# Experts' float32 products written as three products of high and low parts

## The reference

```
hgu = xb @ w_gate_up[e] + b_gate_up[e]
gate, up = jnp.split(hgu, 2, axis=-1)
gate = jnp.minimum(gate, SWIGLU_LIMIT)
up = jnp.clip(up, -SWIGLU_LIMIT, SWIGLU_LIMIT)
act = (up + 1.0) * gate * jax.nn.sigmoid(SWIGLU_ALPHA * gate)
return act @ w_down[e] + b_down[e]
```

## Time and profile before

| | us |
|---|---|
| median of 3 runs | 2881.6 (2881.26 to 2882.64) |
| profiled execution, whole | 2894.67 |
| its span | 2892.9 |
| mean granted TensorE clock in it | 0.948 |

### The profile page before, as it was taken

How to read it: one execution, slowest core, us unless ns; L and a number is a source line. 1 busy time by engine, 2 the same in 40 slices (tenths; PEclk the granted TensorE clock), 3 DMA queues, 4 the chain that set the end, 5 groups by cost and what they waited for, 6 DMA issues and landing times. The chain is left out here.

```text
span 2892.9 us, 47141 instructions
## 1 busy us (share of the span) xinstructions
PE 2727.8 (94%) x18543; PEld 2337.5 (81%) x18544; DVE 1056.3 (37%) x1908; ACT 613.3 (21%) x1272; POOL 242.8 (8%) x214
## 2 busy tenths in 40 slices
PE   7999998786998979999999999999999999999788
PEld 3345543754985559999999999999999999999666
DVE  2143542946242243222223323232323333333365
ACT  2111222325521111111111111111111111111245
POOL 0000001403620000000000000000000000000130
PEclk9999998658999969999999999999999999999889
DMA  3001010000006226677778888899999999999542
GB/s 132 29 30 58 0 62 33 1 22 1 1 19 215 88 84 196 213 234 236 253 257 267 278 265 286 290 296 292 298 295 304 299 309 296 307 298 302 200 158 75
DMA packets 442841, 526.65 MB, mean 182 GB/s; under 512 B 13716, under 2 KB 408808, under 8 KB 442728
## 3 DMA queue, kind: packets, MB, share of 16 engines
q1 hardware_dynamic: 429448, 478.03, 50.4%
q0 software_dynamic: 13280, 46.93, 5.2%
HBM read 486.39 MB, written 38.54 MB: 181 GB/s over the span
## 5 line engine op out<-in xcount | busy, mean ns | idle before, releaser
L1527 PE MATMUL ex_psum<-ex_xT,weight_ring_a 128*128 128x134 f32 (+14 forms) x6144 | 768.9, 286 | 0.8 <-ACT ex_xT L1513 0.8
L1527 PEld LDWEIGHTS ex_psum<-ex_xT,weight_ring_a 128*128 128x128 f32 x6144 | 759.1, 191 | 1.2 <-issue 1.2
L1567 PE MATMUL ex_psum<-ex_hT,weight_ring_b 128*128 128x134 f32 (+14 forms) x4096 | 521.5, 286 | 0.0
L1567 PEld LDWEIGHTS ex_psum<-ex_hT,weight_ring_b 128*128 128x128 f32 x4096 | 508.1, 191 | 0.0
L1537 DVE TENSOR_SCALAR ex_gate<-ex_psum,bias_gate_up 128x192 f32<-128x192 f32 x256 | 95.0, 413 | 696.6 <-PE ex_psum L1527 681.4
L1527 PE MATMUL ex_psum<-ex_xT,weight_ring_b 128*128 128x134 f32 (+14 forms) x2048 | 255.6, 286 | 0.0
L1527 PEld LDWEIGHTS ex_psum<-ex_xT,weight_ring_b 128*128 128x128 f32 x2048 | 252.2, 191 | 0.0
L1541 DVE TENSOR_SCALAR ex_up<-ex_psum,bias_gate_up 128x192 f32<-128x192 f32 x256 | 95.0, 413 | 401.1 <-PE ex_psum L1527 401.1
L239 PE MATMUL project_psum<-nT,w_in_chunks 128*128 128x512 f32 x512 | 225.2, 603 | 3.4 <-DVE nT L358 3.4
L1554 ACT ACTIVATE ex_sig<-ex_gate 128x384 f32<-128x384 f32 x128 | 67.1, 525 | 718.4 <-DVE ex_gate L1537 711.6
L1575 ACT ACTIVATE ex_yT<-ex_psum,bias_down 128x192 f32<-128x192 f32 x256 | 93.8, 418 | 533.0 <-PE ex_psum L1567 533.0
(11 more groups left out here) (313 smaller groups left out, 2908.6 us busy)
## 6 DMA issues: line engine op xcount, KB each, us to landing
weight_ring_a<-in_w_gate_up SPq DMA_DIRECT2D x192, 1024.0 KB, 6.1
weight_ring_b<-in_w_down SPq DMA_DIRECT2D x128, 1024.0 KB, 6.4
weight_ring_b<-in_w_gate_up SPq DMA_DIRECT2D x64, 1024.0 KB, 5.1
y_dram<-ex_y_a SPq DMA_DIRECT2D x33, 512.0 KB, 3.5
w_in_chunks<-in_w_in SPq DMA_DIRECT2D x7, 2048.0 KB, 8.1
y_dram<-ex_y_b SPq DMA_DIRECT2D x33, 256.0 KB, 3.8
project_work<-in_x SPq DMA_DIRECT2D x8, 512.0 KB, 3.7
gates_dram<-project_work POOLq DMA_DIRECT2D x16, 256.0 KB, 2.3
```

The source lines that it names most:

```text
L1527: mm = pe.matmul(self.ps[:, bank, i * CAP:i * CAP + width], w[:, k, i * P:(i + 1) * P], self.xT[:, k, 0:width], start=(k == 0), stop=(k == ...
L1567: mm = pe.matmul(self.ps[:, bank, i * CAP:i * CAP + width], w[:, k, i * P:(i + 1) * P], self.hT[:, k, 0:width], start=(k == 0 and i == 0), ...
```

## The change

Each expert operand exists twice, as a high part (a copy to float32r) and a low part (value minus high part). Every float32 product becomes three float32r products, w_hi by x_hi, w_hi by x_lo and w_lo by x_hi (`pe_product`), and so for h in the down pieces. The host stores the weights piece by piece, so that a partition's 2048 numbers of a piece lie in one run. There are three rings of four pieces: as loaded (`g.raw`), high (`w_hi`, made by ScalarE) and low (`w_lo`, made by VectorE, 1280 or 1024 of the 2048 columns, and by GpSimd, the rest). A piece is loaded when the low part of the piece four before it is made; its high part is made when TensorE has used up the piece four before. x and h are split in the same way by ScalarE and VectorE. TensorE turns y between gate and up pieces, and x in two places before and two between the down pieces. `dve_slots` moves behind the last pass. Freed and taken memory move three loads of `finish` (w_proj and two broadcast rows) into that stage, and w_out of `route` into a tensor of its own.

```diff
-        w_out = g.ring_b[:, 2:6].rearrange("p s n -> p (s n)").rearrange("p (k n) -> p k n", k=KT)
+        w_out = sb("w_out", [P, KT, D])
...
-            for i in range(8):
-                sp.dma_start(ring_slot(g, i).rearrange("p (k n) -> p k n", k=KT), weight_source(g, 0, i)).then_inc(g.w_in_ring[i], 16)
+            for i in range(RING):
+                sp.dma_start(g.raw[:, i], g.w_expert[0, i]).then_inc(g.w_in_ring[i], 16)
...
+RING = 4
+
+LO_CUT = (5 * 256, 4 * 256)
+
+
+def expert_pieces(w_gate_up, w_down):
+
+    up = w_gate_up[0].reshape(E, KT, P, 2, 4, 256).transpose(0, 4, 3, 2, 1, 5).reshape(E, 8, P, 2 * D)
+    down = w_down[0].reshape(E, KT, P, 4, 256).transpose(0, 3, 2, 1, 4).reshape(E, 4, P, 2 * D)
+    return np.ascontiguousarray(np.concatenate([up, down], axis=1))
...
-        self.xT = sb("xT", [P, KT, CAP])
-        self.hT = sb("hT", [P, FF // P, CAP])
+        self.x_hi, self.x_lo = sb("x_hi", [P, KT, CAP], F32R), sb("x_lo", [P, KT, CAP], F32R)
+        self.h_hi, self.h_lo = sb("h_hi", [P, FF // P, CAP], F32R), sb("h_lo", [P, FF // P, CAP], F32R)
+        self.w_hi, self.w_lo = sb("w_hi", [P, RING, 2 * D], F32R), sb("w_lo", [P, RING, 2 * D], F32R)
...
+    def act_x_hi(self, act, x, fill, q, after):
         act.wait_ge(self.turned, fill + q + 1)
-        act.wait_ge(self.gu_done, after)
-        act.copy(self.xT[:, 2 * q:2 * q + 2, :], self.turned_x(q).rearrange("p (i c) -> p i c", i=2)).then_inc(self.turn_kept, 1)
-
-
-    def pe_gate_up(self, pe, m, fill_x, c, width):
-        gate_bank, up_bank = self.GATE_UP[c % 2]
-        if c == 0:
+        if not (isinstance(after, int) and after == 0):
+            act.wait_ge(self.gu_done, after)
+        act.copy(self.x_hi[:, 2 * q:2 * q + 2, :], self.turned_x(q).rearrange("p (i c) -> p i c", i=2)).then_inc(self.x_hi_done, 1)
+
+    def dve_x_lo(self, dve, x, q):
+        cols = slice(2 * q, 2 * q + 2)
+        dve.wait_ge(self.x_hi_done, 4 * x + q + 1)
+        dve.tensor_tensor(self.x_lo[:, cols, :], self.turned_x(q).rearrange("p (i c) -> p i c", i=2),
+                          self.x_hi[:, cols, :].bitcast(F32), ALU.subtract).then_inc(self.turn_kept, 1)
...
+    def act_w_hi(self, act, m, i):
+        act.wait_ge(self.g.w_in_ring[i % RING], 48 * m + 16 * (i // RING + 1))
+        if i >= RING:
+            act.wait_ge(self.gu_done, 8 * m + i - RING + 1)
+        else:
+            act.wait_ge(self.dn_done, 4 * m + i + 1)
+        act.copy(self.w_hi[:, i % RING], self.g.raw[:, i % RING]).then_inc(self.hi_done, 1)
+
+    def w_lo_part(self, eng, m, i, part, done):
+        eng.wait_ge(self.hi_done, 12 * m + i + 1)
+        eng.tensor_tensor(self.w_lo[:, i % RING, part], self.g.raw[:, i % RING, part], self.w_hi[:, i % RING, part].bitcast(F32),
+                          ALU.subtract).then_inc(done, 1)
+
+    def dve_w_lo(self, dve, m, i):
+        self.w_lo_part(dve, m, i, slice(0, LO_CUT[i % 2]), self.lo_dve)
+
+    def pool_w_lo(self, pool, m, i):
+        self.w_lo_part(pool, m, i, slice(LO_CUT[i % 2], 2 * D), self.lo_pool)
+
+    def pe_product(self, pe, out, i, k, slot, hi, lo, width, start, stop):
+        n = slot % RING
+        w_hi, w_lo = (w[:, n].rearrange("p (k n) -> p k n", k=KT)[:, k, i * P:(i + 1) * P] for w in (self.w_hi, self.w_lo))
+        pe.matmul(out, w_hi, hi[:, k, 0:width], start=start, stop=False, skip_group_check=True)
+        pe.matmul(out, w_hi, lo[:, k, 0:width], start=False, stop=False, skip_group_check=True)
+        return pe.matmul(out, w_lo, hi[:, k, 0:width], start=False, stop=stop, skip_group_check=True)
...
-                    mm = pe.matmul(self.ps[:, bank, i * CAP:i * CAP + width], w[:, k, i * P:(i + 1) * P], self.xT[:, k, 0:width],
-                                   start=(k == 0), stop=(k == KT - 1))
...
+                mm = self.pe_product(pe, self.ps[:, bank, i * CAP:i * CAP + width], i, k, slot, self.x_hi, self.x_lo, width,
+                                     k == 0, k == KT - 1)
+        mm.then_inc(self.gu_done, 1)
...
+    def act_h_hi(self, act, m, c):
+        act.wait_ge(self.h_prod, 4 * m + c + 1)
+        act.copy(self.h_hi[:, 2 * c:2 * c + 2, :], self.up[:, c % 2]).then_inc(self.h_hi_done, 1)
+
+    def dve_h_lo(self, dve, m, c):
+        cols = slice(2 * c, 2 * c + 2)
+        dve.wait_ge(self.h_hi_done, 4 * m + c + 1)
+        dve.tensor_tensor(self.h_lo[:, cols, :], self.up[:, c % 2], self.h_hi[:, cols, :].bitcast(F32), ALU.subtract).then_inc(self.h_done, 1)
...
+        def load(sp, e, m, i):
+
+            if i >= RING or not isinstance(m, int):
+                sp.wait_ge(x.lo_dve, 12 * m + i - RING + 1)
+                sp.wait_ge(x.lo_pool, 12 * m + i - RING + 1)
+            src = g.w_expert[bass.ds(e, 1)].rearrange("a i p n -> (a i) p n")[i]
+            sp.dma_start(g.raw[:, i % RING], src).then_inc(g.w_in_ring[i % RING], 16)
...
-            sp.wait_ge(x.gu_done, 8 * (E - 1) + 4)
+            sp.wait_ge(x.lo_dve, 12 * E)
+            sp.wait_ge(x.lo_pool, 12 * E)
...
+            def one_pass(e, last):
+                for i in range(3, 12):
+                    x.pool_w_lo(pool, e, i)
+                    if i == 5:
+                        x.gather(pool, e + 1, 8 * e + 4)
+                if not last:
+                    for i in range(3):
+                        x.pool_w_lo(pool, e + 1, i)
...
+                turn_x = lambda q: x.pe_turn_x(pe, e + 1, 8 * e + 8, q)
                 for c in range(4):
-                    x.pe_gate_up(pe, e, 8 * e + 4, c, width)
+                    x.pe_gate_up(pe, e, 8 * e + 4, c, 0, width)
+                    x.pe_turn_y(pe, 8 * e + 4, 8 * e + 4, c)
+                    x.pe_gate_up(pe, e, 8 * e + 4, c, 1, width)
                     if c == 0:
                         x.pe_list(pe, e + 1)
-                    x.pe_turn_y(pe, 8 * e + 4, 8 * e + 4, c)
-                for c, turns in DOWN_THEN_TURNS:
-                    x.pe_down(pe, e, c, width)
-                    for q in turns:
-                        x.pe_turn_x(pe, e + 1, 8 * e + 8, q)
+                turn_x(0)
+                turn_x(1)
+                x.pe_down(pe, e, 0, width)
+                turn_x(2)
+                x.pe_down(pe, e, 1, width)
+                turn_x(3)
+                x.pe_down(pe, e, 2, width)
+                x.pe_down(pe, e, 3, width)
...
+            def one_pass(m, expert, turn_x, following):
+                x.act_w_hi(act, m, 3)
+                x.act_w_hi(act, m, 4)
+                for c in range(3):
+                    x.act_sigmoid(act, m, c)
+                    x.act_w_hi(act, m, 5 + 2 * c)
+                    x.act_h_hi(act, m, c)
+                    x.act_w_hi(act, m, 6 + 2 * c)
+                x.act_sigmoid(act, m, 3)
+                turn_x(0)
+                x.act_h_hi(act, m, 3)
+                x.act_w_hi(act, m, 11)
+                turn_x(1)
+                for c in range(3):
+                    x.act_down(act, m, expert, c)
+                    if c < 2:
+                        turn_x(2 + c)
+                    following(c)
+                x.act_down(act, m, expert, 3)
...
+            def one_pass(m, expert, keep_y, after_first, turn_x, following):
+                x.dve_w_lo(dve, m, 3)
+                for c in range(4):
+                    x.dve_gate(dve, m, expert, c)
+                    if c >= 1:
+                        x.dve_h_lo(dve, m, c - 1)
+                    keep_y(c)
+                    x.dve_w_lo(dve, m, 4 + 2 * c)
+                    x.dve_up(dve, m, expert, c)
+                    if c == 0:
+                        after_first()
+                    if c < 3:
+                        x.dve_w_lo(dve, m, 5 + 2 * c)
+                x.dve_h_lo(dve, m, 3)
+                turn_x(0)
+                x.dve_w_lo(dve, m, 11)
+                turn_x(1)
+                following(0)
+                turn_x(2)
+                following(1)
+                turn_x(3)
+                following(2)
...
+            for i in range(3):
+                x.dve_w_lo(dve, 0, i)
             x.dve_order(dve)
+            for q in range(4):
+                x.dve_x_lo(dve, 0, q)
...
+            x.dve_find(dve, E, E)
+            one_pass(E - 1, x.expert_at(dve, E - 1), lambda q: x.dve_keep_y(dve, E - 1, 8 * E - 4, q), lambda: x.dve_list(dve, E),
+                     lambda q: x.dve_x_lo(dve, E, q), lambda i: None)
             x.dve_slots(dve)
-            with dve.Fori(0, E) as e:
...
+            sp.dma_start(w_proj[:], g.w_ple_proj.rearrange("a (k p) n -> p (a k) n", p=P)).then_inc(post_in, 16)
+            sp.dma_start(post[:], g.g_ple_post.rearrange("a d -> (a d)").partition_broadcast(P)).then_inc(post_in, 16)
+            sp.dma_start(final[:], g.g_final.partition_broadcast(P)).then_inc(post_in, 16)
...
-            pe.wait_ge(g.ple_in, 64)
+            pe.wait_ge(post_in, 48)
```

(26 more changed lines are left out.)

199 lines of the change are left out of this document (87 added, 112 removed).

## The result

| | before, us | after, us |
|---|---|---|
| median of 4 runs | 2881.4 (2879.4 to 2882.6) | 3976.7 (3949.8 to 4041.2) |
| profiled execution, whole | 2894.67 | 3951.68 |
| its span | 2892.9 | 3949.9 |
| mean granted clock in it | 0.948 | 0.832 |

The kernel became slower, 1.377 times the time of before (interval 1.364 to 1.390). The direction was forecast. The time was not: 3445 us, and 3640 at most. Unlike before, the runs of the changed kernel scatter by over 2%, the longer ones with the lower mean clock (0.810 in the longest, 0.830 in the shortest), and the ratio is taken without the longest.

A forecast was written before the change was run, and what follows sets the result against it. TensorE's records bound the experts' stage, each new one costing its weight load. The profiled 2894.7 + 553 products + 10 start + 2 end = 3460, less 13.1 for the median: 3447, say 3445 us; range 3340 to 3640.

The forecast's parts named there:

- What bounds it: Experts' stage: costs what TensorE's instruction stream costs, matmuls and weight loads busy all the time in narrow passes.
- Products, +553 us: Experts' stage: 18432 records at 111.5 ns for every width, one weight load each, 2055 us against 1502.
- Rival D: Experts' products: a new product with few columns streams more than once; twice gives +673, 3565 us; chance 0.05.
- Rival A: Experts' products: new loads are short or hidden, a record costs 73 ns at mean width; 2790 us; chance 0.09.
- The clock: Experts' stage: granted clock expected to stay 1.00; a fall to the lower level was considered only as a rival.
- Rival B: Experts' stage: granted clock at the lower level throughout, a load 210 ns; +2369, about 5260 us; chance 0.03.
- Preparation, 0: Experts' passes: copies and subtractions on ScalarE (39 us), VectorE (37) and GpSimd (29) hide under 68.3 us passes; zero cost.
- rival C: Experts' passes: hand-overs at pass edges or the VectorE and GpSimd SBUF port cost 4 us each; +128, 3575; chance 0.08.
- The start, +10 (5 to 15): Before the experts' first product: w_lo and x_lo work on VectorE delays it from 1081.5 to near 1092; +10 us.
- The end, +2: Last stage: w_proj and two broadcast rows load in it instead of before; +2 us (0 to 9.4).
- The weights' DMA: Experts' passes: 12 MB per 68 us is 184 GB/s where 301 is moved now; zero cost.

The follow-up runs named there:

- the bfloat16 kernel with the new cut: The changed kernel with operands split into bfloat16 parts, and VectorE making 1984 of each w_lo piece's 2048 columns, GpSimd 64: 2854.4 us.

## Why the prediction was right in its sum and wrong in its time

- **What bounds it**: right. TensorE's records set the stage before and after, and it waits for nothing in it.
- **Products, +553 us**: right. 18432 records, 112 ns at 182 columns as at 192 and at 128, where 111.5 was taken. Rival D (streams twice) is out: 192 columns twice would be 160 ns. Rival A is out for this type, and its mechanism is shown for bfloat16.
- **The clock**: this is the step that failed. Rival B was stated for the whole stage only, at 5260 us and 0.03, so that a fall in a part of it, 7.8 of 32 passes, had no case and no place in the range. Its counter-argument was the router's 16 records, which streamed 27 of 106 ns and kept the pace for 1.7 us. The row was too short to carry that: the changed kernel itself ran its passes of 124 columns and the start of the first of 120, 148 us, at 1.00 before the clock fell. A better row was at hand in the forecast's own working. The narrow passes before stream 90 of 111 ns, those after 45 to 52. That was a state of the engine that no row before covered, and its price (a floor of 210 ns, measured 213.7) was known. No row told in which passes the clock would fall; but for the eight narrowest alone, a choice that is made with hindsight, the forecast's own figures give 4608 x (210 - 111.5) = 454 us, with 33 for their transposes +487, and 3932 us, 1% under the measured time.
- **Preparation, 0**: right in passes of 68 us, for a reason that was half wrong. From the window at 2400 to 2600, per pass of 68.3 us: ScalarE 33 us (39 forecast), VectorE 44 (37), GpSimd 41 (29). The last two take turns, and their times have grown by the waiting for each other, which the forecast's figures, read where each worked alone, did not hold. "If TensorE took under 40 us per pass, ScalarE would be late next" fell: with one float32 product, where TensorE's own work is 47 to 66 us a pass as before, it already stood idle for 142 us, and what it waited for was VectorE's. So rival C's mechanism is real (206 us in that stage, 6 a pass), but a pass of 68 us covers it. Rival A's 2790, which gave back 50 us for this, came out as 2969 in bfloat16, where its mechanism holds.
- **The start, +10 (5 to 15)**: it was 15.8. From VectorE's first operation of the stage to the first product it is 35.5 us (1063.53 to 1099.02) instead of 19.7 (1061.89 to 1081.54), and 35.5 again in the kernel without passes under 128 columns; the other 1.6 of the 17.5 belong to the stages ahead. Of the excess of 5.8, 5.3 us are one operation on 32 columns, 0.18 us before, that lay behind GpSimd's three w_lo pieces. It reads one tensor only, as L1581 above does, so operations with a single input in SBUF are held too:

```profile
1077.61 5.87 POOL L1536 TENSOR_TENSOR ex_w_lo<-weight_ring,ex_w_hi 128x768 fp32r<-128x768 f32 x3
1078.08 5.44 DVE L1436 TENSOR_SCALAR ex_base<-ex_rank 128x32 f32<-128x32 f32 x1
```

- **The end, +2**: it was 6. **The weights' DMA**: as forecast, no wait for it.

## What to carry to other kernels

Count weight loads, not columns, when products are narrow: splitting float32 into three one-pass products adds a load per product, and with float32r that load is as dear as float32's. Before a change makes TensorE stream less of the time, look for a row that shows the clock in that state for as long as the new state will last; if there is none, the lower clock in exactly those stretches is a case with its own price, not a remote one. And work given to an idle GpSimd is not free for VectorE: try it with nearly nothing on GpSimd.

## What the runs showed that was not expected

- The granted clock fell to 0.50 while TensorE's weight loads were back to back and nothing waited. With these products it held in passes of 128 columns (3000 to 3200 us, 1.00), went and came in those of 124, stayed at 0.50 in those of 120 to 108 and came back 5 us after the first product of 192. The Trainium skill, TensorE: Matmul & The Clock Gate, section Part 1: The HAM clock gate (the "warmup" mystery), says that activity releases the throttle; these runs show that a full stream of loads with narrow products behind it did not hold it. Whether the two-column products of the list trigger the fall stays open.
- A GpSimd subtraction of 64 elements still took 1.36 us on average in the bfloat16 kernel with the new cut (busy us, mean ns, idle before); at its fastest it is 297 ns, so most of it is the wait for its turn at the port:

```profile
L1536 POOL TENSOR_TENSOR ex_w_lo<-weight_ring,ex_w_hi 128x64 bf16<-128x64 f32 x384 | 520.6, 1361 | 910.9 <-ACT ex_w_hi L1532 909.9
...
L1536 POOL TENSOR_TENSOR ex_w_lo<-weight_ring,ex_w_hi x384: 297/1140/2392, 1077.9 to 2668.1; 128x64 bf16<-128x64 f32 x192
```

- Contiguous pieces brought the DMA engines only from 93 to 84% busy at the same rate.
